# One 512-column product for both parts of x in six weight slabs of a hybrid trunk

## The reference

```
even layer:  aq, af, ai, bq, bk, bv, z = split(h)
   oa = gated linear recurrence of (aq, af, ai), 8 heads of 128
   ob = softmax attention of rotary(bq), rotary(bk), bv; causal, 8 heads of 128
        (rotary turns the first 32 of 128 features)
   x += (concat(oa, ob) * silu(z)) @ w_out
odd layer:   cx, dq, dk, dv, z = split(h)
   oc = gated recurrence over conv4(cx): causal convolution of width 4 per channel
   od = retention of rotary(dq), rotary(dk), dv
   x += (concat(oc, od) * silu(z)) @ w_out
after each:  x += cross attention(rms_norm(x), memory)
```

## Time and profile before

| | us |
|---|---|
| median of three runs | 586.78 |
| span of the profiled execution, first to last instruction | 584.0 |
| TensorE busy | 575.8 |
| VectorE busy | 416.3 |
| ScalarE busy | 384.3 |
| GpSimd busy | 73.8 |

### The profile page before, as it was taken

One profiled execution on the slowest core, in us unless ns is written; L12 is line 12 of the kernel. 1 busy time (PEld: TensorE's weight loads), 2 busy tenths in 40 slices (PEclk: granted clock), 3 DMA queues, 4 the chain that ended last, 5 costly groups with the idle time before them and its releaser, 6 DMA issues.

```text
span 584.0 us, 9717 instructions
## 1 busy us (share of the span) xinstructions
PE 575.8 (99%) x3868; PEld 532.9 (91%) x3868; DVE 416.3 (71%) x647; ACT 384.3 (66%) x581; POOL 73.8 (13%) x77
## 2 busy tenths in 40 slices
PE   8999999999999999999999999999999999999995
PEld 7999989999999898889988999999899998888985
DVE  6879589447977684567557874799997974766663
ACT  6863685278397575657666847969758837566764
POOL 4130005001003900100000001112120200100002
PEclk9999999999999999999999999999999999999999
DMA  9856354446715963564445545326544463356201
GB/s 290 255 181 227 108 181 145 145 145 216 218 72 162 289 200 144 177 229 172 145 145 176 184 162 181 128 109 224 208 145 145 167 233 133 118 217 220 105 2 72
DMA packets 51856, 98.88 MB, mean 169 GB/s; under 512 B 1732, under 2 KB 7140, under 8 KB 51812
## 3 DMA queue, kind: packets, MB, share of 16 engines
q1 hardware_dynamic: 50628, 96.95, 49.2%
q0 software_dynamic: 1024, 1.05, 0.7%
q10 hardware_dynamic: 160, 0.27, 0.1%
HBM read 96.16 MB, written 1.05 MB: 166 GB/s over the span
## 4 chain that ended last, share of the span: by engine, by line
PE 97%; DMA 1%; DVE 1%; ACT 0%; issue 0%; SPq 0%; DVEq 0%; ACTq 0%
PE proj L1775 17%; PE proj L1776 17%; PE proj L1777 17%; PE proj L1794 11%; PE proj L1795 11%; PE proj L1796 11%; PE head L2010 4%; PE head L2086 1%; PE head L2193 1%; PE head L1854 1%; DMA x_residual<-in_x_dram 1%; PE head L1987 1%; PE head L2055 1%; PE head L2224 1%; PE head L2095 1%; PE proj L1816 0%
## 5 line engine op out<-in xcount | busy, mean ns | idle before, releaser
L1090 DVE TENSOR_TENSOR w_lo<-raw_weights,w_hi 128x1024 fp32r<-128x1024 f32 x174 | 224.3, 1304 | 105.9 <-ACT w_hi L515 104.2
L515 ACT ACTIVATE w_hi<-raw_weights 128x1024 fp32r<-128x1024 f32 x174 | 182.1, 1056 | 118.1 <-PE proj L1777 60.5
L1775 PE MATMUL proj<-xT_hi,w_hi 128*128 128x256 f32 x752 | 215.9, 287 | 0.0
L1777 PE MATMUL proj<-xT_hi,w_lo 128*128 128x256 f32 x752 | 212.8, 283 | 0.0
L1776 PE MATMUL proj<-xT_lo,w_hi 128*128 128x256 f32 x752 | 212.7, 283 | 0.0
L1775 PEld LDWEIGHTS proj<-xT_hi,w_hi 128*128 128x128 f32 x752 | 144.2, 192 | 0.6
L1776 PEld LDWEIGHTS proj<-xT_lo,w_hi 128*128 128x128 f32 x752 | 144.2, 192 | 0.5
L1777 PEld LDWEIGHTS proj<-xT_hi,w_lo 128*128 128x128 f32 x752 | 144.2, 192 | 0.0
L1794 PE MATMUL proj<-w_hi,y_hi 128*128 128x512 f32 x176 | 69.4, 394 | 0.0
L1796 PE MATMUL proj<-w_lo,y_hi 128*128 128x512 f32 x176 | 68.5, 389 | 0.0
L1795 PE MATMUL proj<-w_hi,y_lo 128*128 128x512 f32 x176 | 68.5, 389 | 0.0
(11 more groups left out here) (297 smaller groups left out, 775.6 us busy)
## 6 DMA issues: line engine op xcount, KB each, us to landing
raw_weights<-in_ev_w_in_dram SPq DMA_DIRECT2D x15, 2048.0 KB, 8.6
raw_weights<-in_od_w_in_dram SPq DMA_DIRECT2D x12, 2048.0 KB, 7.9
raw_weights<-in_ev_w_out_dram SPq DMA_DIRECT2D x4, 2048.0 KB, 7.7
raw_weights<-in_xa_wkv_dram SPq DMA_DIRECT2D x4, 2048.0 KB, 7.6
raw_weights<-in_od_w_out_dram SPq DMA_DIRECT2D x4, 2048.0 KB, 7.8
raw_weights<-in_xa_wq_dram SPq DMA_DIRECT2D x2, 2048.0 KB, 9.2
raw_weights<-in_xa_wo_dram SPq DMA_DIRECT2D x2, 2048.0 KB, 8.3
x_residual<-in_x_dram SPq DMA_DIRECT2D x2, 512.0 KB, 3.8
```

Of the source, the lines that this page charges most:

```text
L515: act.activation(ring_quarter(w_hi, n, q), raw_quarter(n, q), ACT.Copy).then_inc(hi_ready, 1)
L1090: dve.tensor_tensor(ring_quarter(w_lo, n, q), raw_quarter(n, q), ring_quarter(w_hi, n, q).bitcast(F32), ALU.subtract).then_inc(lo_ready, 1)
L1775: pe.matmul(dst, wh[:, k, :], x_hi[:, k, :], start=(k == 0), stop=False)
L1777: last = pe.matmul(dst, wl[:, k, :], x_hi[:, k, :], start=False, stop=(k == KC - 1))
```

## The change

A slab kind X is new, for q and k of stage B and x of stage C, in both groups: 6 slabs. xT_hi and xT_lo become two planes of one tensor xT, and the four proj banks one tensor. A quarter of kind X has a bank of its own: the left half takes the hi weights times xT_hi plus the lo weights times xT_hi, the right half the hi weights times xT_lo. One matmul of 512 columns does both products with the hi weights. An X slab has two turns, so both pairs: quarters 0 and 1 the first, 2 and 3 the second. ScalarE copies the left halves of a pair, VectorE adds the right halves to that copy and releases the pair. In stage B the packed rows are then read from the sum in SBUF.

More of the change, by code:

```diff
@@ L57 @@
 for _g in range(2):
-    SLABS += [("C", "x", "F", _g), ("C", "z", "F", _g)]
+    SLABS += [("C", "x", "X", _g), ("C", "z", "F", _g)]
 for _g in range(2):
@@ L142, in hybrid_trunk @@
         kx = scan_mask[:, :].rearrange("p (h t) -> p h t", h=4)
-        proj = [ctx.enter_context(nc.psum_tensor(f"proj{i}", [P, 512], F32)) for i in range(4)]
+        proj_banks = ctx.enter_context(nc.psum_tensor("proj", [P, 4, 512], F32))
+        proj = [proj_banks[:, i, :] for i in range(4)]
         head = [ctx.enter_context(nc.psum_tensor(f"head{i}", [P, 512], F32)) for i in range(4)]
@@ L220, in hybrid_trunk @@
         o_rstd = sem("o_rstd")
+        q_halves = sem("q_halves_copied")
+        q_summed = sem("q_summed")
+        k_halves = sem("k_halves_copied")
+        k_summed = sem("k_summed")
         q_rows = sem("q_rows_copied")
@@ L286, in raw_quarter @@
             r = raw[:, n % 2, :]
-            if kind == "F":
+            if kind in "FX":
                 return r.rearrange("p (k c) -> p k c", k=KC)[:, :, P * q:P * q + P]
@@ L294, in ring_quarter @@
         def ring_quarter(ring, n, q):
-            return ring[:, q, :].rearrange("p (k c) -> p k c", k=KC if SLABS[n][2] == "F" else 2)
+            return ring[:, q, :].rearrange("p (k c) -> p k c", k=KC if SLABS[n][2] in "FX" else 2)
         def bank(n, u, half=0):
@@ L308, in filled, with bank_halves @@
                 return
-            eng.wait_ge(quarter_used, 4 * n + (2 * u + 2 if kind == "F" else 2 * half + 2 if kind == "W" else 4))
+            eng.wait_ge(quarter_used, 4 * n + (2 * u + 2 if kind == "F" else 2 * half + 2 if kind in "WX" else 4))
+        def bank_halves(n, half, w):
+            pair = 2 * ((TURN[n] + half) % 2)
+            return proj_banks[:, pair:pair + 2, S * w:S * w + S]
         def y_src(i):
@@ L688, in softmax_exp, with halves_copied, packed_rows @@
                                    accum_out=st[:, 32 + c:33 + c]).then_inc(probs, 1)
[L690 to L698, removed]
+            def halves_copied(n, half, w, s):
+                filled(act, n, 1, half)
+                act.activation(blocks(w)[:, 2 * half:2 * half + 2, :], bank_halves(n, half, 0), ACT.Copy).then_inc(s, 1)
+            def packed_rows(g, half, w, summed, s):
+                act.wait_ge(summed, 2 * g + half + 1)
+                if w == 0 and half == 0:
+                    act.wait_ge(k_ready, g)
+                for h in (2 * half, 2 * half + 1):
+                    last = act.activation(packed[32 * h:32 * h + 32, 2 * w, :], blocks(w)[0:32, h, :], ACT.Copy)
+                last.then_inc(s, 1)
             def stage_b(g):
@@ L715, in stage_b @@
                     rstd_a(1)
+                packed_rows(g, 1, 0, q_summed, q_rows)
                 ahead(k, 2)
-                turn_rows_packed(k, 0, 1, k_rows)
+                halves_copied(k, 0, 1, k_halves)
                 ahead(k, 3)
@@ L720, in stage_b @@
                     y_high(1)
+                packed_rows(g, 0, 1, k_summed, k_rows)
                 ahead(v, 0)
-                turn_rows_packed(k, 1, 1, k_rows)
+                halves_copied(k, 1, 1, k_halves)
                 ahead(v, 1)
+                packed_rows(g, 1, 1, k_summed, k_rows)
                 ahead(v, 2)
@@ L933, in rows @@
                 def rows(u):
-                    filled(act, cx, u)
+                    filled(act, cx, 1, u)
                     if g:
                         act.wait_ge(xf_ready, 2 * g)
-                    act.activation(cxp[:, 2 * u:2 * u + 2, 3:S + 3], bank(cx, u)[:].rearrange("p (h t) -> p h t", h=2),
-                                   ACT.Copy).then_inc(cx_ready, 1)
-                    act.drain().then_inc(free_of(cx, u), 1)
+                    act.activation(cxp[:, 2 * u:2 * u + 2, 3:S + 3], bank_halves(cx, u, 0), ACT.Copy
+                                   ).then_inc(cx_ready, 1)
                 ahead(cx, 0)
@@ L1779, in quarter_f, with slab_x @@
                     last.then_inc(quarter_used, 1)
+            def quarter_x(n, q, norm=None):
[4 more added lines that the diff above has]
+                both = dst.rearrange("p (w t) -> p w t", w=2)
+                wh, wl = ring_quarter(w_hi, n, q), ring_quarter(w_lo, n, q)
+                for k in range(KC - 1):
+                    if norm is not None:
+                        pe.wait_ge(xT_lo_ready, KC * norm + k + 1)
+                    pe.matmul(both, wh[:, k, :], xT[:, :, k, :], start=(k == 0), stop=False)
+                    pe.matmul(dst[:, 0:S], wl[:, k, :], xT_hi[:, k, :], start=False, stop=False)
+                if norm is not None:
+                    pe.wait_ge(xT_lo_ready, KC * norm + KC)
+                pe.matmul(dst[:, 0:S], wl[:, KC - 1, :], xT_hi[:, KC - 1, :], start=False, stop=False)
+                pe.matmul(both, wh[:, KC - 1, :], xT[:, :, KC - 1, :], start=False, stop=True).then_inc(quarter_used, 1)
+            def slab_x(n, qs=range(4), norm=None):
+                for q in qs:
+                    quarter_x(n, q, norm=norm if q == 0 else None)
             def quarter_t(n, q, x_hi, x_lo, k0, half=0, start=True, stop=True):
@@ L2199, in stage_c @@
                 cx, z = slab("C", "x", g), slab("C", "z", g)
-                slab_f(cx, norm=2 if g == 0 else None)
+                slab_x(cx, norm=2 if g == 0 else None)
                 slab_f(z)
```

8 lines of the change are left out of this document (4 added, 4 removed).

## The result

The changed kernel takes 592.83 us (592.40 to 593.58) where the kernel before took 586.81 in the same set of runs: +6.0 us, ratio 1.0102 with a 95% interval of 1.0082 to 1.0122. Slower, as forecast (593.6, range 589.9 to 596.0).

What follows compares the result with a forecast made beforehand. TensorE was taken as the bound, busy 575.8 of 584.0 us. Pause +5.5, stage C wait +0.45, savings -1.50 and clock +2.4 sum to +6.85 on the 586.78 median: 593.6 us, range 589.9 to 596.0 (8 in 10).

Steps and rivals of the forecast that it cites:

- The pause: Stage B, group 1, query quarter 2: TensorE waits for ScalarE to release the bank pair, starting +5.5 us later, about 5.3 idle.
- VectorE's delay passed on to ScalarE: Stage B, group 0: sums of k delay the rotation and row maxima, so ScalarE's work up to the SiLUs moves 0.95 us.
- The clock: Behind the pause TensorE runs 4.9 us of work at half speed, as at the kernel's start: +2.4 us, bounds 0 and 2.5.
- The saving of a quarter: In the changed slabs each quarter saves 107 ns through fused pairs; 14 quarters from the pause on give -1.50 us.
- Waits inside group 0 of B: TensorE waits 0.6 us at v's quarter 3 and another 0.6 at the scores; neither reaches the end.
- z of stage C's group 1: z waits for the bank pair whose halves VectorE sums behind its split: +0.45 us, bounds 0 and 0.9.
- All else behind the pause has slack: The rest of B's second group is released by then, and other stage C places have slack; nothing counted.
- The 2.8 us between the span before and the median: Time before the first and after the last instruction, taken as unchanged between the profiled span and the median of runs.
- the kept clock: Rival: TensorE's clock stays at 2.4 GHz through the pause, +4.45, 591.2 us; chance 0.33.
- the operand priced as two products: Rival: the wide product's two-run operand costs as much as two products, nothing saved, 595.3 us; chance 0.08.
- a free bank: Rival: the pair of B's z is free when group 1's query quarter 2 is due, 585.9 us; chance 0.04 (faster).

Runs made afterwards that it cites:

- act_late: The changed kernel with one more ScalarE copy of 1024 columns ahead of the SiLUs that empty z of stage B's group 0; 594.45 us.
- no_sums: The changed kernel without stage B's additions of the right halves, with waits, drains and releases kept; 593.16 us (591.66 to 594.45).
- filler14: The changed kernel with 14 unused fp32 products of 128 columns on TensorE in the pause before quarter 2 of group 1's queries; 590.85 us, ratio 1.0063.
- grouped: The changed kernel with a quarter's seven wide products in a row, then the seven narrow ones and the last pair; 593.49 us.
- q_narrow: The changed kernel with the query slab of stage B's group 1 in its old form (256-column products, one pair of banks); 588.32 us, ratio 1.0029.
- silu_early: The changed kernel with the SiLUs that empty z of stage B's group 0 moved ahead of the memory rows' squares and the probabilities' copies; 593.39 us.
- filler: The changed kernel with 28 unused fp32 products of 128 columns on TensorE in the pause before quarter 2 of group 1's queries; 593.60 us.

## Why the prediction was right, step by step

- **The pause** (+5.5 forecast at quarter 2): the shift there is +5.41, TensorE went on at ScalarE's release, and act_late moved it one for one. Right in place, cause and size. TensorE came to it 1.0 us late, so its wait was 4.2 us and not the 5.3 that the prediction named as the sign.
- **VectorE's delay passed on to ScalarE** (0.95): the first exponential is 161.19-0.60-159.79 = 0.80 late. no_sums gives the sums 0.57 of it. Right, a little too large. The release is 1.64-0.60 = 1.04 late; the step from 0.80 is the unexplained gap on ScalarE, so that 0.95 comes so near to 1.04 is luck.
- **The clock** (+2.4 forecast): the mechanism was right, the size too large. The quarter took 182.46-177.98 = 4.48 us for 2.81, so 1.67; filler14 gives 1.5 to 2.0. The slow stretch lasted 3.6 us, not the 4.9 of the kernel's start. In grouped, behind the same pause, the quarter took 5.3 us, a loss of about 2.5: the forecast's size does occur, but not in the profiled run of the changed kernel.
- **The saving of a quarter** (107 ns): 67 ns. The term was mis-sized. The price of a wide product was taken from a stream of equals, and it runs here between narrow ones; that is about half of the difference (grouped), the rest is open. Over 14 quarters -0.9 instead of -1.5.
- **Waits inside group 0 of B** (0.6 at v's quarter 3, 0.6 at the scores): wrong. There is one, 1.4 us, at v's first product, and none at the scores. The step that failed is that in stage B only the slab in front of a wide slab was asked after, though at z of stage C's group 1 the slab behind was too: a slab behind a wide one takes the pair of its first half, two quarters after that was filled, not four. v needs the pair of k's first half, and VectorE sums that at 140.65 behind the recurrence's gate, while TensorE stands there from 140.0. Silu_early shows the same at k behind q. As forecast, nothing before the pause reached the end, so the error cost nothing; in q_narrow it does.
- **z of stage C's group 1** (+0.45): over that group the shift stays where 4 quarters should have given -0.27, so +0.27. The right place and cause, within the bounds: z's first product follows at the end of VectorE's sum (377.28+0.69 = 377.97), 0.44 us behind x's last one instead of 0.23.

```profile
377.28 0.69 DVE L1609 TENSOR_TENSOR work<-proj,work 128x512 f32<-128x512 f32 x1
377.61 0.39 PE L1837 MATMUL proj<-xT,w_hi 128*128 128x512 f32 x1
378.05 0.39 PE L1815 MATMUL proj<-xT,w_hi 128*128 128x256 f32 x1
```

- **All else behind the pause has slack**: right for the changed kernel, and q_narrow and silu_early show by how much: waits of 1.4 us in the one and 4.2 in the other appear once the pause is gone.

The sum was +6.85, the shift at stage D's scores is +6.36, and the medians differ by 6.02. That the total is so near is in part luck: the clock's term was about 0.8 too large and the saving 0.6 too large, and the two nearly cancel. The 2.8 us between the span before and the median are not a constant either: in every run with both numbers the time is 1.7 to 2.3 us above the span, and the profiled execution of before was a short one. The forecast adds to the median, so this does not touch it. Of the rivals, the kept clock (591.2) is refuted by the granted 0.57, the operand priced as two products by the 67 ns, and a free bank by the pause.

## What to carry over

When a tile takes twice the banks, ask of both neighbours how long the buffer has to come free: the slab in front loses half its time to be emptied, and so does the wide slab itself before the one behind. Then read on the emptying engine's timeline which steps are tied behind the waiting engine's own last work; that gives a floor for the wait that no speed-up lifts. A saving of nanoseconds per instruction must be priced in the sequence in which it will run, and a pause of a saturated TensorE is to be charged with the slow products behind it as well, as a range: behind the same pause they cost 1.7 us in one kernel's trace and 2.5 in another's.

## What the hardware showed that was not expected

- After 4.2 us of idle the granted clock was 0.57 over the next four microseconds; in silu_early 0.63 followed on two waits of 1.79 and 2.37 us, 8 us apart. The 1.41 us before v and the 0.84 us in filler14 were not followed by a fall.
- The low clock behind the same pause did not last equally long: a quarter of 2.8 us took 4.5 us in the changed kernel and 5.3 in grouped, and the four runs of no_sums fall in two pairs 2.4 us apart with different mean clocks.
- A 512-column fp32r product takes 227 ns in a stream of its like, 230 in a row of seven, and 234 between products of 256 columns, and the latter two whether its operand is one run or two. The 256-column products between them take 117 instead of 120.
- An fp32 product of 128 columns appears as two instructions of 0.112 us: 28 products in filler, 56 rows in 6.27 us (174.21 to 180.48).
